# A transpose in place of the second product of each inverse level, in the delta-rule blocks of a two-layer encoder

## What is computed

```python
proj = h @ w_in                                  # all columns of both mixers
a = tril(k_beta @ k.T * decay, -1) + I           # per chunk and head
sol = triangular_solve(a, [v_beta, k_beta*exp(g)])
v_new = u - w @ state
o = q_dec @ state + attn @ v_new
out_a = rmsnorm(o) * silu(z)                     # mixer A
out_b = gelu(u_raw) * (w_s @ layernorm(gelu(v_raw)))   # mixer B
x = x + concat(out_a, out_b) @ w_out
```

## Time and profile before

| | |
|---|---|
| median of 3 runs | 2178.35 us (2175.86 to 2178.73) |
| the profiled execution | 2179.36 us, span 2177.6 us |
| TensorE busy | 98% of the span |
| VectorE, ScalarE busy | 71%, 54% |
| granted TensorE clock, mean | 0.993 |

### The profile page before, as it was taken

The page is one execution under the profiler, slowest core; times in us unless marked ns, Lnnn a source line. Parts: engine busy times, 40 slices in busy tenths (PEclk is TensorE's granted clock), DMA queues, the critical chain, the costliest instruction groups (busy, mean ns, idle before and its releaser), DMA issues.

```text
span 2177.6 us, 37662 instructions
## 1 busy us (share of the span) xinstructions
PE 2123.5 (98%) x14180; PEld 1982.0 (91%) x14180; DVE 1545.6 (71%) x1531; ACT 1165.5 (54%) x1461; POOL 37.5 (2%) x56
## 2 busy tenths in 40 slices
PE   7999999999999999999999999899999999999997
PEld 7999998999999999999999999799999999999997
DVE  7757647667766766766777889978665765765766
ACT  5644445545555545555554888765444444544454
POOL 0000000000000000000000012000000000000000
PEclk9999999999999999999999999999999999999999
DMA  6544334466777878778778866255666666666664
GB/s 227 176 125 128 111 111 141 131 210 213 269 271 275 284 265 283 267 277 287 262 283 299 325 239 245 78 192 197 209 198 199 203 196 207 195 202 203 196 206 139
DMA packets 127878, 464.18 MB, mean 213 GB/s; under 512 B 14496, under 2 KB 14880, under 8 KB 127776
## 3 DMA queue, kind: packets, MB, share of 16 engines
q1 hardware_dynamic: 112608, 408.22, 56.4%
q10 hardware_dynamic: 14400, 52.44, 6.1%
q0 software_dynamic: 768, 2.10, 0.5%
HBM read 427.04 MB, written 35.65 MB: 212 GB/s over the span
## 4 chain that ended last, share of the span: by engine, by line
PE 85%; DVE 11%; ACT 2%; issue 1%; DMA 1%; DVEq 0%; SPq 0%; ACTq 0%
PE ps L1267 42%; PE ps L1269 21%; PE ps L1242 4%; PE ps L1244 4%; PE ps L1246 4%; PE ps L1396 3%; DVE rest L1082 2%; PE ps L1338 2%; DVE wlo L742 2%; DVE work L1105 1%; DVE rest L1090 1%; PE ps L1391 1%; ACT whi L355 1%; PE ps L1317 1%; PE ps L1319 1%
## 5 line engine op out<-in xcount | busy, mean ns | idle before, releaser
L742 DVE TENSOR_TENSOR wlo<-raw,whi 128x1024 fp32r<-128x1024 f32 x672 | 818.4, 1223 | 401.6 <-ACT whi L355 384.7
L355 ACT ACTIVATE whi<-raw 128x1024 fp32r<-128x1024 f32 x672 | 708.6, 1057 | 571.4 <-PE ps L1269 497.3
L1267 PE MATMUL ps<-hid,whi 128*128 128x512 f32 x2240 | 734.5, 382 | 1.8 <-DVE hid L1172 1.8
L1267 PE MATMUL ps<-xg,whi 128*128 128x512 f32 x2048 | 671.8, 382 | 0.4 <-ACT sq_part L401 0.4
L1269 PE MATMUL ps<-hid,wlo 128*128 128x256 f32 x2240 | 610.6, 273 | 0.0
L1269 PE MATMUL ps<-xg,wlo 128*128 128x256 f32 x2048 | 558.2, 273 | 0.0
L1267 PEld LDWEIGHTS ps<-hid,whi 128*128 128x128 f32 x2240 | 423.3, 189 | 61.7 <-issue 2.7
L1267 PEld LDWEIGHTS ps<-xg,whi 128*128 128x128 f32 x2048 | 387.1, 189 | 54.5 <-ACT sq_part L401 0.7
L1269 PEld LDWEIGHTS ps<-hid,wlo 128*128 128x128 f32 x2240 | 430.1, 192 | 0.0
L1269 PEld LDWEIGHTS ps<-xg,wlo 128*128 128x128 f32 x2048 | 393.2, 192 | 0.1
L1242 PE MATMUL ps<-xg,whi 128*128 128x256 f32 x768 | 221.7, 289 | 12.1 <-DVE wlo L742 12.1
(11 more groups left out here) (236 smaller groups left out, 2033.2 us busy)
## 6 DMA issues: line engine op xcount, KB each, us to landing
raw<-in_wts SPq DMA_DIRECT2D x704, 512.0 KB, 4.7
pre_raw<-in_pw ACTq DMA_DIRECT2D x32, 512.0 KB, 10.2
pw_hi<-pre_hi ACTq DMA_DIRECT2D x32, 512.0 KB, 6.8
pw_lo<-pre_lo ACTq DMA_DIRECT2D x32, 512.0 KB, 8.4
whi<-pw_hi SPq DMA_DIRECT2D x32, 512.0 KB, 5.2
wlo<-pw_lo SPq DMA_DIRECT2D x32, 512.0 KB, 6.1
x<-in_xt SPq DMA_DIRECT2D x4, 512.0 KB, 8.4
x<-in_xt ACTq DMA_DIRECT2D x4, 512.0 KB, 6.1
```

The lines of the kernel that those rows point to most:

```text
L355: nc.scalar.activation(whi[:, i % SPLIT].rearrange("p a b -> p (a b)"), raw[:, r, HALF * (i % 2):HALF * (i % 2) + HALF], ACT.Copy).then_in ...
L742: tt(wlo[:, i % SPLIT].rearrange("p a b -> p (a b)"), raw[:, i // 2 % RAW, HALF * (i % 2):HALF * (i % 2) + HALF], whi[:, i % SPLIT].rearra ...
L1267: mm(ps[:, 4 * par + n, :], whi[:, r, k, cols], woven_parts(operand[:, kt]), start=(kt == 0), stop=False)
```

## The change

Each level computes only U by products. T is made by transposing the new U after ScalarE has copied it. A level has three steps in place of two: Y, U, and the transposes of U. ScalarE makes two copies of 512 columns per level in place of one of 1024. The last level makes no T, as before. Blocks are 36 parts apart and no longer 33, and the steps up to the levels are moved closer together: `gb` 7 parts behind `tok` (8 before), `t_prod` one part behind `attn` (2 before), the first level one behind `t_prod` as before. The blocks start at parts 59, 95, 131 and 167 (59, 92, 125, 158 before); `o` of the last one is at part 201 (189 before).

```diff
 NEVER = 1 << 30
 
 
-GATES_START, BLOCK_START, BLOCK_TIME = 32, 59, 33
-AT = {"tok": 0, "gb": 8, "feat": 10, "attn": 12, "t_prod": 14, "levels": 15, "w": 27, "v": 28, "s": 29, "o": 31}
+GATES_START, BLOCK_START, BLOCK_TIME = 32, 59, 36
+AT = {"tok": 0, "gb": 7, "feat": 9, "attn": 11, "t_prod": 12, "levels": 13, "w": 30, "v": 31, "s": 32, "o": 34}
 UV_ROWS, UV_MIX = 6, 12
 NARROW_BANK = [0, 2] * 6 + [0, 4, 6, 4]
 UNSPLIT = G_PW2 - G_PW1
@@ -485,15 +485,16 @@
                     if m:
                         copy(buf["qdT"], bank(5)).then_inc(s["feat_act"], 1)
                     yield start + AT["t_prod"]
-                    act.wait_ge(s["t_prod"], b + 1)
+                    act.wait_ge(s["t_prod"], LEVELS * b + 1)
                     copy(buf["T"], bank(5)).then_inc(s["t_copy"], 1)
-                    for lev in range(1, LEVELS):
-                        yield start + AT["levels"] + 2 * lev - 1
+                    for lev in range(1, LEVELS + 1):
+                        yield start + AT["levels"] + 3 * lev - 2
                         act.wait_ge(s["ut_prod"], LEVELS * b + lev)
-                        copy(ut, ps[:, 4:6, :]).then_inc(s["t_copy"], 1)
-                    yield start + AT["levels"] + 2 * LEVELS - 1
-                    act.wait_ge(s["ut_prod"], LEVELS * b + LEVELS)
-                    copy(buf["U"], bank(4)).then_inc(s["u_copy"], 1)
+                        copy(buf["U"], bank(4)).then_inc(s["u_copy"], 1)
+                        if lev < LEVELS:
+                            yield start + AT["levels"] + 3 * lev - 1
+                            act.wait_ge(s["t_prod"], LEVELS * b + lev + 1)
+                            copy(buf["T"], bank(5)).then_inc(s["t_copy"], 1)
                     if m:
                         yield start + AT["w"]
                         act.wait_ge(s["w_prod"], hh + 1)
@@ -942,7 +943,7 @@
                     dve.wait_ge(s["attn"], b + 1)
                     tt(buf["attnT"], bank(4), buf["decay"], ALU.mult).then_inc(s["attn_copy"], 1)
                     for lev in range(1, LEVELS + 1):
-                        yield start + AT["levels"] + 2 * lev - 2
+                        yield start + AT["levels"] + 3 * lev - 3
                         dve.wait_ge(s["y_prod"], LEVELS * b + lev)
                         tt(buf["Z"], bank(6), all_heads(const(f"lev{lev}")), ALU.mult).then_inc(s["z"], 1)
                     yield start + AT["s"]
@@ -1436,19 +1437,20 @@
                     pe.wait_ge(s["inv0"], b + 1)
                     transposes(5, lambda h: buf["U"][:, h, :]).then_inc(s["t_prod"], 1)
                     for lev in range(1, LEVELS + 1):
-                        yield start + AT["levels"] + 2 * lev - 2
+                        yield start + AT["levels"] + 3 * lev - 3
                         pe.wait_ge(s["t_copy"], LEVELS * b + lev)
                         products(6, buf["C"], buf["T"]).then_inc(s["y_prod"], 1)
-                        yield start + AT["levels"] + 2 * lev - 1
+                        yield start + AT["levels"] + 3 * lev - 2
                         pe.wait_ge(s["z"], LEVELS * b + lev)
                         if lev == 1:
                             pe.wait_ge(s["attn_copy"], b + 1)
-                        ins = products(4, buf["Z"], buf["U"])
+                        products(4, buf["Z"], buf["U"]).then_inc(s["ut_prod"], 1)
                         if lev < LEVELS:
-                            ins = products(5, buf["U"], buf["Z"])
-                        ins.then_inc(s["ut_prod"], 1)
+                            yield start + AT["levels"] + 3 * lev - 1
+                            pe.wait_ge(s["u_copy"], LEVELS * b + lev)
+                            transposes(5, lambda h: buf["U"][:, h, :]).then_inc(s["t_prod"], 1)
                     yield start + AT["w"]
-                    pe.wait_ge(s["u_copy"], b + 1)
+                    pe.wait_ge(s["u_copy"], LEVELS * (b + 1))
                     if m:
                         products(5, buf["kd"], buf["U"]).then_inc(s["w_prod"], 1)
                         pe.wait_ge(s["state"], hh + 1)
```

## The result

| | before | changed |
|---|---|---|
| median of 10 runs each | 2177.98 us | 2182.57 us |
| lowest and highest | 2175.86, 2178.73 | 2181.47, 2184.88 |
| profiled execution: its time, its span | 2179.36, 2177.6 | 2183.37, 2181.6 |
| TensorE busy | 2123.5 | 2115.2 |

The ratio is 1.0023, with a 95% interval of 1.0015 to 1.0032: the changed kernel is slower by 4.6 us (3.3 to 7.0). Against the median shown with the prediction (2178.35) that is +4.2, where the forecast said 2181.5; the time lies 1.1 above it and within the range.

A forecast was written before the change was run, and what follows sets the result against it. TensorE was taken to bound the kernel (busy 314.5 of 334.0 us); cheaper work, waits removed and waits added summed to +3.2 us, 2182.6 against the profiled execution or 2181.5 against the median, range 2174 to 2188.5.

The forecast's parts named there:

- step 2: Regular TensorE waits for Z in blocks 0 and 2 go: -4.1 us; +11 if every level still loses 0.65.
- Step 1: TensorE's work in 20 levels: transposes at 0.36 + 0.08 us replace products at 0.90, in all -9.2.
- Steps 3 and 6: Gelu no longer delaying Z -4.6; two before T's copy +3.3; Silus, groups 3, 4, 6: +4.1, +1.6, +1.55 us.
- Step 5: `gb` of block 0: TensorE comes one part earlier, norms ready as before, +1.35 us on top of 1.8.
- Step 7: `feat` of block 1 waits for VectorE as `tok` falls into the convolution: 4.5 us lost for 2.4, +2.1.
- Step 8: Mixer B's steps in the levels of blocks 2 and 3 take ScalarE's time ahead of a copy: +2.0 us.
- Step 9: Mixer B's round 1 (part 172) waits for VectorE's norms: 5.1 us lost and a clock drop, net +4.5.
- Step 10: End of mixer A (part 201): output projection loses 5.1 us and a clock drop, +6.8; mixer B catches up, -4.05.
- Step 11: The other last steps of blocks: 2.6 us lost in place of 3.1, -0.5.
- rival of drops at the waits of 1.55 to 1.7: Clock drops behind five middle waits: two drops give +6.6 us, all five +11.7; chance 0.25.
- rival of a costlier table load: Each ScalarE table switch costs 2.66 us, not 1.28, where something waits: +10.8 us, 2189.2; chance 0.03.
- Cheaper collisions: VectorE is ready at mixer B's round 1 and mixer A's end: -8.1 us, 2170.2; chance 0.17.

The follow-up runs named there:

- experiment 1: Kernel before, put in the new order (36-part blocks, three parts a level) but keeping its two products and one wide copy: 2191.51 us, ratio 1.0061.
- experiment 10: experiment 8 with T made by a second product and one wide copy in place of the transposes: 2181.09 us, ratio 1.0021.
- experiment 2: Changed kernel with mixer B's round 1 moved behind the norms of `tok` (transposes at part 170, product at 175): 2181.68 us, ratio 1.0017.
- experiment 7: experiment 5 with the product of mixer B's round 1 moved from part 172 to 175: 2174.97 us, ratio 0.9990.
- experiment 5: Changed kernel with all four blocks two parts earlier (57, 93, 129, 165): 2175.58 us, ratio 0.9988.
- experiment 6: Kernel before with its blocks two parts earlier (57, 90, 123, 156), two products, 33 parts: 2192.93 us, ratio 1.0062.
- experiment 8: experiment 7 with mixer B's round 3 starting two parts earlier (196) and its product at 203 for 204: 2173.60 us, ratio 0.9979.
- experiment 4: Transposes in the order of the kernel before: 33-part blocks, two steps a level, transposes in U's own slot: 2183.74 us, ratio 1.0028.

## Why the prediction was right

It was right in its mechanism: the cheaper work, the waits that go and those that come are where it put them. That the median came out only 1.1 us from the forecast is in part luck, since errors in the clock and in step 2 met each other, and 1.5 us of the span came where the two programs are the same.

The waits below are the recorded idle; from start to start they cost about 0.2 us more, which is what the forecast calls lost.

- **Step 1, TensorE's work (-9.2):** the account of the stretch gives -9.2 with the clock taken out, and experiments 1 and 10 give 8.3 and 9.1 by the ratios.
- **Step 2, the regular waits (-4.1):** they are gone, in blocks 0 and 2 too, and +11 is ruled out. But the term was too large by about 1 us. In the kernel before the seven short waits cost 0.46 to 0.54 us each ahead of U, and 0.10 each because U behind a wait takes 0.99 us to the next start and otherwise 0.89: 4.3 in all, not 4.6. And eight U of the changed kernel still start 0.19 to 0.27 us behind the matmul ahead of them, where 0.11 is the step without a gap, and take 0.91 to the next start for 0.82. They have no number in brackets, and cost 1.8 us together. One of them:

```profile
152.11 0.28 PE L1247 MATMUL ps<-xg,wlo 128*128 128x256 f32 x1
152.30 1.16 PE L1397 MATMUL ps<-x_space,work 128*128 128x128 f32 x8
```

The kernel before has three such, 0.6 us. So step 2 was worth -4.3 + 1.8 - 0.6 = -3.1: the chain that I had found about 0.1 us late costs 0.2 us and more where it is late. The 0.19 that step 2 adds to each wait was a misreading: that is the first step of any part behind a product, with or without a wait, and what a wait adds is the 0.10.
- **Steps 3 and 6, Gelus and Silus:** the two Gelus 1.46 each for 1.65; block 0's first level 2.29 for 2.4; the Silus of groups 4 and 6 1.31 and 1.52 for 1.6 and 1.55 (the second ends at 246.18). The drop that I put behind the 2.4 did not come.
- **Step 5, gb of block 0:** 3.15 us, exactly 1.8 + 1.35. But the drop that the kernel before has there (1.7 us) is not in the changed kernel's trace, and I had carried it over.
- **Step 7, feat of block 1:** 4.37 for 4.5.
- **Step 8, mixer B in the levels (+2.0):** 1.13 at 314.04 and 0.55 at 393.30, 1.7 us.
- **Step 9, round 1 (+4.5):** 5.07 for 5.1, but the low clock behind it lost 2.9 us and not 1.7.
- **Step 10, end of mixer A (+6.8, -4.05):** 4.99 for 5.1, with 2.2 of clock for 1.7, mixer B's product without a wait, its last result 1.70 for 1.7 and no drop behind it.
- **Step 11:** four waits of 0.55 to 0.56, 2.2 us for 2.6.

So the longer waits came where the order of the queues put them, within 0.3 us each. What failed is the rule of the clock, a drop of 1.7 us on every wait of recorded idle over 1.8. By it the changed kernel had five drops, 8.5 us, for four before, 6.8, and so +1.7. The traces have 6.6 for 6.8, -0.2: two drops fewer than forecast, and two that were larger. Without it the sum would be +3.2 - 1.9 = +1.3, where the stretch shows +2.5; 1.0 of the 1.2 left over is step 2, as shown above.

The rival of drops at the waits of 1.55 to 1.7 is out: in twelve traces none of those had one. The rival of a costlier table load is out as well: the two Gelu waits lose 1.63 and 1.62 us from start to start, the 1.65 that goes with a load of 1.28. Cheaper collisions are out by steps 9 and 10. Of the median's +4.6, the stretch of one execution explains 2.5, and 1.0 and 0.5 are at places where the two programs are the same. The 0.6 that is left is no part of the change in these two executions: the profiled one of the kernel before stood 1.4 above its median and that of the changed kernel 0.8 above its own. What moves a kernel between executions is for the most part the clock, as the last section shows. Whether the changed kernel loses more to it than the kernel before on average is not shown: the profiled execution had full speed behind the waits of 3.15 and 2.29, and one that has a low clock behind both would take 3.4 us more; experiment 1, which waits the same 3.15 and 2.29 us, has it behind both.

## What to carry to other kernels

Replacing work by cheaper work on the bound engine paid its full TensorE price here (0.42 to 0.46 us a level, in either order), and the order that it needed cost more than that; price the two apart and look for a better place of the whole before dropping the change, since here 9 us lay in a few starting numbers. A wait behind an engine that works in order and almost without a gap may only move when the step that waits is moved: 5.07 us became 3.01 + 0.57 + 1.48 in experiment 2, and 3.43 became 4.95 elsewhere in experiment 7. The long waits could be forecast from the order of the two queues to 0.3 us, where the order was worked out in full; where it was not, in the expectations for experiments 5 to 8, waits of 2 to 5 us came unforeseen. What the clock adds behind a wait could not be forecast: it was nothing or up to 1.7 us behind waits of 1.8 to 3.3 us, and 1.4 to 2.9 behind longer ones.

## What the hardware showed that I had not expected

The same wait, of the same length and at the same place, is followed by a low clock in one execution and not in another. Ahead of `gb` of block 0, the wait of 3.15 us in experiment 1, with the 2.29 of its first level (windows of 6 us behind each):

```profile
120.72:126.72 6.00, 6.00 (x34) 4.86 (x35) 3.66 (x5) 2.42 (x4) 0.00 (x0) 0.74 0.27 87
139.46:145.46 6.00, 6.00 (x39) 6.00 (x40) 1.22 (x1) 1.97 (x2) 0.00 (x0) 0.72 0.28 87
```

In the changed kernel both are at 1.00 (above). The wait of 1.81 us has 0.72 behind it in the kernel before, and in experiment 4:

```profile
122.17:128.17 6.00, 6.00 (x48) 5.47 (x49) 4.11 (x6) 3.46 (x4) 0.00 (x0) 1.00 0.29 87
```

And experiments 5 and 7, which are the same program up to there, behind 2.67 us. Experiment 5, then 7:

```profile
196.45:202.45 6.00, 6.00 (x54) 6.00 (x55) 5.86 (x10) 3.34 (x4) 0.00 (x0) 1.00 0.40 117
```

```profile
196.89:202.89 6.00, 6.00 (x39) 6.00 (x40) 5.86 (x10) 3.33 (x5) 0.00 (x0) 0.72 0.38 109
```

Over the twelve traces, between 100 us and the end of mixer B, by the recorded idle of the wait:

| recorded idle | waits | with a low clock behind | lost each |
|---|---|---|---|
| 1.0 to 1.71 | 55 | 0 | - |
| 1.81 to 3.27 | 46 | 24 | 1.4 to 1.7 |
| 3.43 to 5.09 | 16 | 16 | 1.4 to 2.9 |

In the middle row the length says little: 1.81 has it and 3.15 has it not. What tells the cases apart is not in what I read. The waits of a row are not independent: many are the same wait, seen in several related programs. A drop can also begin late: behind the wait that ends at 308.17 in the kernel before, the first eight matmuls take their usual 1.16 us and only then the clock falls (1.00 up to 309.33, 0.50 from 309.50), so that a glance at the first instruction behind a wait is not enough. Or it begins early: in the changed kernel the clock is at 0.50 from 432 us on, and the wait ends at 434.10. For a forecast I would price a wait of the middle row at its length plus about half of 1.7 us, as 24 of 46 had the drop. For a measurement it means that a kernel with four such waits has executions up to 6.8 us apart. The runs of the kernel before range from 2174.38 to 2179.94, and they go with the clock: over its 82 runs beside the experiments the time and the mean granted clock of a run have a correlation of -0.82. The 18 runs at 0.996 or 0.997 have a median of 2175.2 us, the 56 at 0.994 or below 2178.5.
